# A 21st weight slot under the attention masks, the last projection items in two parts of 256 columns, and router products straight by token

## The chip, the core and the metric

The kernel runs on one core of a Trainium2 chip, in one launch. The metric is the device time of the program in microseconds (us), the median of the runs shown; lower is better. Inputs and weights are float32 in the device's memory (HBM), and the output is written back there.

## The reference

Two layers over 256 tokens of width 1024. Each layer first mixes tokens in three parallel branches and adds the result to x, then runs a mixture of experts on the new x. What matters here is the last projection, the router behind it, and the weights of 32 experts:

```python
merged = (gates[:, :, 0] * (oa @ w_proj_a[l]) + gates[:, :, 1] * (ob @ w_proj_b[l])
          + gates[:, :, 2] * (oc @ w_proj_c[l]))
x = x + merged @ w_out[l]                                 # w_out: 1024 x 1024
x = x + hier_moe(rms_norm(x, norm2_g[l]), w_router_group[l], w_router_expert[l],
                 w_expert_gate[l], w_expert_up[l], w_expert_down[l])

def hier_moe(h, w_rg, w_re, w_gate, w_up, w_down):        # h: 256 tokens x 1024
    pg = softmax(t @ w_rg)                                # 4 groups: the best one
    le = t @ w_re                                         # 8 experts in it: the best two
    hg, hu = t @ w_gate[e], t @ w_up[e]                   # 32 experts, each 1024 x 256
    return sum(silu(hg) * hu * weight @ w_down[e])        # and 256 x 1024
```

One expert's three matrices are 1 MB each, so a layer reads 96 MB of expert weights. Before the experts each layer reads some 46 MB for its projections.

## The kernel before

**Two stages in each layer.** The trunk (`trunk_stage`) does norm, projections and attention. The expert stage (`expert_stage`) does the router, then the experts in eight quads of four. Layer 0's trunk takes about the first 315 us, its expert stage lasts to about 524, and layer 1 repeats the two.

**The trunk's products.** Weights come in items of 1 MB through a ring of four slots in `arena`. An item is worked through in two half items, numbered j, so j = 88 to 91 are the last two items of `w_out` (items 44 and 45). To keep float32 accuracy, each half item is split: ScalarE (ACT) writes the rounded part `whi` (L811), VectorE (DVE) the remainder `wlo` in two halves (L991), and TensorE (PE) does three passes, L1295 to L1297. The half items of the last projection are `project_halves(84, 8, 4, ...)`: columns 0 to 511 of both token blocks first (j = 84 to 87), then columns 512 to 1023 (j = 88 to 91), twelve products of 512 columns each. When a block of 128 tokens by 512 columns is done, `x_out` adds it to `xs` (L1237) and raises `x_done`.

**The router.** `turn_new_x` (L545) transposes the new x, 8 transposes for each half of the columns. ACT and DVE scale the result into `h2t` (L521, L528). `router_half` (L556) multiplies the router weights `wr`, 64 columns wide and held in the array, by `h2t`, with even and odd blocks of k in the two halves of the array. This gives logits by expert, transposed, in two partial sums. DVE copies them (`logits_t`, L1633), and two products with `fold` (L1595) turn them by token and add the halves. `keep_clock` (L338) fills PE's time while DVE picks the experts (up to `sel`, L1655); the ranks follow (L1601 to L1606), then the one-hot tables, the gather of tokens (L1784, later L1824) and the gate and up products (L1797, later L1849; in the last quad L1871).

**The 20 slots of expert weights.** 12 slots lie in `arena` and 8 in `ring_rest`. The load number pos goes into slot pos % 20. The first 16 loads are issued inside the trunk as its data become free (`load_ahead`, by hand, between the projection items), four more when the last projection is done. From load 20 on (`quads_sp`, L470) each waits until the quad that used its slot is done: the first of them waits for `gate_up_pair(0)`. All these loads, and those of the trunk, are issued by SyncE (SP) in program order and share one queue. The last four loads of a layer are the down matrices of the last quad. The fourth comes in two halves, and `down_last` (L1889) multiplies in the order 0, 1, 2, 3. Right behind them in the queue stand the next layer's first items.

**The masks.** `mask_a` and `mask_c` are 1536 floats per partition, made once in layer 0 by DVE (L389 to L396) and read by the softmax of both layers (L1097). After the last softmax of layer 1 the final norm's gain is loaded into the same place.

## Time and profile before

| what | value |
| --- | --- |
| runs | 1054.49, 1053.40, 1053.19 us, median 1053.4 |
| profiled execution | 1054.47 us, of which the profile's span is 1052.8 |
| PE busy | 961.5 us (91% of the span) |
| DVE, ACT busy | 578.1 us (55%), 425.5 us (40%) |
| HBM read, written | 309.42 MB, 1.05 MB |
| granted TensorE clock, mean | 0.969 of 2.4 GHz |

Times in the rows further down are us from the start of the span. PE is the matmul engine and PEld its weight loads, which run beside the products. SPq is SyncE's sequencer while it issues a DMA; such a row tells when the transfer was issued and not when it landed. A record of PE is one pass: a float32 product or transpose of the text may be one or two records. "x8" behind a row is a merged run of eight. The bracket behind a row is the engine's idle time before it and what ended it.

### The profile page before, as it was taken

The page shows a single profiled execution, that of the slowest core. Times are in us where ns is not written, and L with a number is a line of the kernel's source. Part 1 is how long each engine was busy: PE and PEld are TensorE (multiplying, and loading weights), DVE is VectorE, ACT ScalarE, POOL GpSimd, SP SyncE. Part 2 cuts the span into 40 slices and gives each one's busy share as a digit, 9 for nine tenths or more (in the row PEclk, how much of TensorE's full clock was granted, in tenths as well). Part 3 has the DMA queues.
Part 4 walks back from the last instruction along what each step waited for, and adds up shares of the span by engine and source line. Part 5 has one row for each costly group of instructions (what it writes and reads, how often), then busy time and mean ns, then how long its engine had stood idle before and what let it go on. Part 6 is the DMA issues. An engine that isn't in the chain of part 4 may idle for free.

```text
span 1052.8 us, 15163 instructions
## 1 busy us (share of the span) xinstructions
PE 961.5 (91%) x5782; PEld 657.0 (62%) x5782; DVE 578.1 (55%) x1187; ACT 425.5 (40%) x905; POOL 58.5 (6%) x75
## 2 busy tenths in 40 slices
PE   8999999999999986977999999999999999776696
PEld 6788777777876432533588887777788754332343
DVE  7766788886864321211276568898869632122212
ACT  5434566666434110210353355666664421101122
POOL 1120400000010000000003004000000100000000
PEclk9999999999999998988999999999999999998898
DMA  9965544146899999999997664441569999999996
GB/s 339 349 203 184 188 126 135 62 129 237 306 408 401 420 421 416 419 421 421 409 381 239 198 199 160 125 137 61 154 225 379 418 388 421 421 419 419 421 420 257
DMA packets 96824, 311.43 MB, mean 296 GB/s; under 512 B 13392, under 2 KB 18544, under 8 KB 74224
## 3 DMA queue, kind: packets, MB, share of 16 engines
q1 hardware_dynamic: 96416, 310.47, 78.0%
q8 instruction: 43, 0.70, 0.3%
q14 instruction: 29, 0.24, 0.1%
q10 hardware_dynamic: 336, 0.02, 0.0%
HBM read 309.42 MB, written 1.05 MB: 295 GB/s over the span
## 4 chain that ended last, share of the span: by engine, by line
PE 63%; DMA 15%; SPq 8%; DVE 7%; ACT 4%; issue 3%; DVEq 0%; POOLq 0%; ACTq 0%
PE ps L1295 14%; PE ps L1297 14%; PE ps L1296 14%; DMA arena<-in_w_expert_up_dram 10%; SPq L470 7%; PE ps L1849 5%; DMA ring_rest<-in_w_expert_down_dram 5%; PE ps L1824 2%; PE ps L1393 2%; PE ps L1913 2%; DVE wlo L991 2%; PE ps L1401 2%; PE ps L1797 1%; ACT probs L886 1%; PE ps L1925 1%
## 5 line engine op out<-in xcount | busy, mean ns | idle before, releaser
L991 DVE TENSOR_TENSOR wlo<-arena,whi 128x512 fp32r<-128x512 f32 (+1 forms) x368 | 248.3, 714 | 98.1 <-ACT whi L811 95.7
L1295 PE MATMUL ps<-whi,ahi 128*128 128x512 f32 (+1 forms) x736 | 292.2, 397 | 6.6 <-DVE wlo L991 5.0
L1296 PE MATMUL ps<-wlo,ahi 128*128 128x512 f32 (+1 forms) x736 | 283.6, 385 | 0.0
L1297 PE MATMUL ps<-whi,alo 128*128 128x512 f32 (+1 forms) x736 | 283.5, 385 | 0.0
L811 ACT CAST whi<-arena 128x1024 fp32r<-128x1024 f32 (+1 forms) x184 | 189.1, 1030 | 200.6 <-PE ps L1297 199.7
L1295 PEld LDWEIGHTS ps<-whi,ahi 128*128 128x128 f32 x736 | 138.2, 188 | 41.9 <-DVE wlo L991 10.2
L1297 PEld LDWEIGHTS ps<-whi,alo 128*128 128x128 f32 x736 | 138.2, 188 | 28.4
L1296 PEld LDWEIGHTS ps<-wlo,ahi 128*128 128x128 f32 x736 | 138.5, 188 | 24.9
L1849 PE MATMUL ps<-ring_rest,rows 128*32 128x512 f32 x320 | 99.4, 669 | 30.2 <-DMA arena<-in_w_expert_up_dram 30.2
L1849 PE MATMUL ps<-arena,rows 128*32 128x512 f32 x448 | 99.4, 683 | 12.7 <-DMA arena<-in_w_expert_up_dram 7.5
L2041 DVE SCALAR_TENSOR_TENSOR acts<-ps,wslot,acts 128x256 f32<-128x256 f32 x16 | 7.7, 484 | 171.3 <-ACT acts L1759 148.0
L1759 ACT ACTIVATE acts<-ps,rslot 128x256 f32<-128x256 f32 x16 | 7.6, 475 | 171.4 <-PE ps L1849 168.5
L1824 PEld LDWEIGHTS ps<-onehot,work 128*128 128x128 f32 x448 | 53.4, 199 | 22.1 <-DVE onehot L2000 13.7
L1824 PE MATMUL ps<-onehot,work 128*128 128x128 f32 x448 | 56.0, 285 | 12.1 <-DVE onehot L2000 12.1
L1849 PEld LDWEIGHTS ps<-ring_rest,rows 128*32 128x32 f32 x320 | 23.7, 121 | 66.8 <-issue 66.8
L886 ACT ACTIVATE probs<-probs,neg 128x128 f32<-128x128 f32 x112 | 49.6, 444 | 33.1 <-DVE neg L1114 33.1
L1925 PE MATMUL ps<-rows,st 128*128 128x512 f32 x112 | 54.9, 612 | 0.2
L1849 PEld LDWEIGHTS ps<-arena,rows 128*32 128x32 f32 x448 | 24.4, 123 | 45.1 <-issue 45.1
L2025 DVE TENSOR_TENSOR xs<-ps,xs 128x512 f32<-128x512 f32 x56 | 38.7, 692 | 22.7 <-PE ps L1925 22.7
L1010 DVE SCALAR_TENSOR_TENSOR arena<-ps,rstd,arena 128x512 f32<-128x512 f32 (+2 forms) x68 | 46.7, 728 | 2.2 <-PE ps L1297 2.2
L1913 PE MATMUL ps<-arena,acts 128*32 128x512 f32 x256 | 43.6, 595 | 3.7 <-ACT acts L1763 3.7
L1913 PE MATMUL ps<-ring_rest,acts 128*32 128x512 f32 x192 | 36.3, 595 | 2.8 <-ACT acts L1763 2.8
(280 smaller groups left out, 970.2 us busy)
## 6 DMA issues: line engine op xcount, KB each, us to landing
arena<-in_w_in_dram SPq DMA_DIRECT2D x62, 1024.0 KB, 5.3
arena<-in_w_expert_gate_dram SPq DMA_DIRECT2D x36, 1024.0 KB, 25.5
arena<-in_w_expert_down_dram SPq DMA_DIRECT2D x32, 1024.0 KB, 22.8
arena<-in_w_expert_up_dram SPq DMA_DIRECT2D x32, 1024.0 KB, 26.2
ring_rest<-in_w_expert_down_dram SPq DMA_DIRECT2D x30, 1024.0 KB, 14.0
ring_rest<-in_w_expert_up_dram SPq DMA_DIRECT2D x24, 1024.0 KB, 27.2
ring_rest<-in_w_expert_gate_dram SPq DMA_DIRECT2D x20, 1024.0 KB, 26.5
arena<-in_w_proj_a_dram SPq DMA_DIRECT2D x8, 1024.0 KB, 5.0
```

The costliest lines, as they stand in the source:

```text
L470: sp.dma_start(slot, w[l, 4 * n + e].rearrange("(p k) f -> p (k f)", p=P)).then_inc(done, 16)
L811: act.copy(whi[:, jj % 2, 0:2 * w], half_slot(jj, w)).then_inc(hi_ready, 1)
L886: act.activation(probs[:, i, n, lo:hi], probs[:, i, n, lo:hi], ACT.Exp, bias=neg[:, i, tb, n:n + 1], accum_out=den[:, i, tb, n:n + 1])
L991: dve.tensor_tensor(wlo[:, jj % 2, cols], half_slot(jj, w)[:, cols], whi[:, jj % 2, cols].bitcast(F32), ALU.subtract).then_inc(low_split i ...
L1010: dve.scalar_tensor_tensor(out=z[:, tb, cols], in0=ps[:, bank + tb, 0:w], scalar=rstd[:, tb:tb + 1], in1=z[:, 0, cols], op0=ALU.mult, op1= ...
L1295: pe.matmul(o, hi, rhs_hi, start=first, stop=False)
L1296: pe.matmul(o, hi, rhs_lo, start=False, stop=False)
L1297: return pe.matmul(o, lo, rhs_hi, start=False, stop=last)
L1824: mm = pe.matmul(ps[:, 4 + k // 4, (k % 4) * QUAD:(k % 4 + 1) * QUAD], work[:, tb, k * P:(k + 1) * P], onehot[:, n % 2, tb, :], start=(tb ...
L1849: mm = pe.matmul(ps[e * EC:(e + 1) * EC, n % 2, :].rearrange("p (a f) -> p a f", a=2), xsel[:, k, e * EC:(e + 1) * EC], w, start=(k == 0), ...
L1913: mm = pe.matmul(ps[e * EC:(e + 1) * EC, 2 + nh, :], at_sb[:, kf, e * EC:(e + 1) * EC], w, start=(kf == 0), stop=(kf == 1), skip_group_che ...
L1925: pe.matmul(ps[:, 4 + tb, :], st[:, n % 2, tb * P:(tb + 1) * P], y[:, nh * BANK:(nh + 1) * BANK], start=True, stop=True).then_inc(R.back_r ...
```

## The change

The masks move into `spare_slot`, a buffer the size of one weight slot. In layer 0 the finished masks are written to device memory (`mask_store`). From the last softmax on, the buffer takes the down matrix of the layer's last expert; in layer 1 the masks are read back at the start of the trunk, and the cycle repeats. That load, number 95, leaves the end of the layer's queue. `down_last` takes it first, and the third matrix now comes in two halves. The gain of the final norm goes to an arena slot.

The load into slots 0 and 1 is issued at item 39 and no longer at item 42. The columns 512 to 1023 of the last projection are done as two parts of 256 columns, each through both items: j = 88, 89 for the first part, 90, 91 for the second, 24 products of 256 columns each. New x is therefore ready in steps (`x_done` 1 and 2, then 3 and 4, then 5 and 6), and it is transposed and sent to the router in parts of 4, 2 and 2 blocks of k (`X_PARTS`). The router products hold `h2t` in the array and stream the 36 columns of `wr`, so that logits come out by token; the copy, `fold` and its products go. `keep_clock` has one matmul less in two places.

```diff
-        mask_a = sb("mask_a", [P, 384])
-        mask_c = sb("mask_c", [P, 3, 384])
+        spare_slot = sb("spare_slot", [P, SLOT])
+        masks = spare_slot[:, 0:4 * 384]
+        mask_a = masks[:, 0:384]
+        mask_c = masks[:, 384:].rearrange("p (g c) -> p g c", g=3)
+        mask_store = nc.dram_tensor("mask_store", [P, 4 * 384], F32, kind="Internal").ap()
...
+        wr = sb("wr", [P, KB, WR])
...
+        gf = arena_slots[:, PLACES[16], 0:D]
...
+        WARM_SETUP, WARM_ROUTE, WARM_RANKS, WARM_LAST = 7, 7, 1, 1
...
+        def last_place(e):
+
+            return spare_slot[:] if e == 3 else places((LAST_DOWN - 3 + e) % RING_E)[:, 0, :]
+
         def load_last_down(sp, l, e):
 
-            slot = places((LAST_DOWN - 3 + e) % RING_E)[:, 0, :]
+            slot = last_place(e)
             src = w_expert_down[l, EXPERTS - 4 + e].rearrange("(p k) f -> p (k f)", p=P)
-            if e < 3:
+            if e != 2:
                 sp.dma_start(slot, src).then_inc(last_in[e], 16)
                 return
             for kf in range(2):
-                sp.dma_start(slot[:, kf * D:(kf + 1) * D], src[:, kf * D:(kf + 1) * D]).then_inc(last_in[3 + kf], 16)
+                sp.dma_start(slot[:, kf * D:(kf + 1) * D], src[:, kf * D:(kf + 1) * D]).then_inc(last_in[2 + 2 * kf], 16)
...
 
+        NARROW = 88
+
+        def turned_new(k):
+
+            bank = 5 if k == KB - 1 else 4 + k // 2
+            at = 0 if k == KB - 1 else (k % 2) * S
...
-        def turn_new_x(pe, nh):
-            pe.wait_ge(x_done, 2 * nh + 2)
-            for k in range(4 * nh, 4 * nh + 4):
+        X_PARTS = (range(0, 4), range(4, 6), range(6, 8))
+
+        def turn_new_x(pe, part):
...
+                pe.wait_ge(x_done, 2 * part + tb + 1)
+                for k in X_PARTS[part]:
+                    mm = pe.transpose(turned_new(k)[:, tb * P:(tb + 1) * P], xs[:, tb, k * P:(k + 1) * P], ident[:])
+                    if tb and k % 2:
+                        mm.then_inc(x_turned, 1)
...
+                pe.wait_ge(ahead_in, 16 * 3)
+            for k in X_PARTS[part]:
+                if k == 2 or k == KB - 1:
+                    pe.wait_ge(h2t_odd, 1 if k == 2 else 2)
+                elif k % 2 == 0:
+                    pe.wait_ge(h2t_ready, part + 1)
                 for tb in range(TB):
-                    at = (k % 2) * S + tb * P
-                    mm = pe.transpose(ps[:, 4 + k // 2, at:at + P], xs[:, tb, k * P:(k + 1) * P], ident[:])
...
-                               skip_group_check=True)
-            if nh:
-                mm.then_inc(logits_t_ready, 1)
+                    mm = pe.matmul(ps[:, 4, tb * 64:tb * 64 + WR], h2t[:, k, tb * P:(tb + 1) * P], wr[:, k, 0:WR],
+                                   start=(k == 0 and tb == 0), stop=(k == KB - 1), skip_group_check=True)
+            if part == 2:
+                mm.then_inc(logits_ready, 1)
...
-                ENDS = {71: 2, 75: 4, 77: 8, 80: 10, 83: 12, 87: 14}
+                ENDS = {71: 2, 75: 4, 77: 8, 80: 10, 83: 12, 87: 14, 89: 16}
...
+                            sp.wait_ge(before_me.y_ready, 2 * QUADS)
+                            sp.dma_start(masks, mask_store).then_inc(masks_in, 16)
+                        else:
+                            sp.wait_ge(masks_made, 1)
+                            sp.dma_start(mask_store, masks).then_inc(masks_out, 16)
...
+                                if l == 0:
+                                    sp.wait_ge(masks_out, 16)
+                                load_last_down(sp, l, 3)
                             if item == 38:
                                 sp.wait_ge(sv_ready, 1)
                                 sp.wait_ge(pv_mm, turned_before(BATCHES))
                                 load_ahead(18, 19)
+                            if item == 39:
+                                sp.wait_ge(obt_ready, 3)
+                                sp.wait_ge(o_lo, 5)
+                                load_ahead(0, 1)
                             if item == 42:
-                                sp.wait_ge(obt_ready, 3)
                                 sp.wait_ge(gated, 4)
-                                load_ahead(0, 1, 2)
+                                load_ahead(2)
                             if item == 43:
                                 sp.wait_ge(gated, 8)
                                 load_ahead(6, 4, 5)
...
                         load_ahead(11)
...
+                        sp.wait_ge(low_split, NARROW + 3)
                         load_ahead(8)
-                        sp.wait_ge(low_split, 2 * 46)
+                        sp.wait_ge(low_split, NARROW + 4)
                         load_ahead(9, 10)
...
+                            dve.wait_ge(masks_in, 16)
                         softmax_in(0)
...
+                        def x_narrow(c, tb):
+                            dve.wait_ge(quarter_ready, 14 + 2 * c + tb + 1)
+                            cols = slice(c * (BANK // 2), (c + 1) * (BANK // 2))
+                            to = quarter(xs, 2 + tb)[:, cols]
+                            dve.tensor_tensor(to, ps[:, 2 - 2 * c + tb, 0:BANK // 2], to, ALU.add).then_inc(x_done, 1)
...
+                        x_narrow(0, 0)
+                        x_narrow(0, 1)
                         low_at(91)
                         h2t_dve(dve, l, 1)
-                        x_out(2)
-                        x_out(3)
+                        x_narrow(1, 0)
+                        x_narrow(1, 1)
 
...
-                            for i in range(2 * pairs):
+                        def project_narrow(kb0, between):
+
+
+                            for i in range(4):
+                                j, (c, item) = NARROW + i, divmod(i, 2)
+                                if i in between:
+                                    between[i]()
+                                for kk in range(2):
+                                    pe.wait_ge(low_split if kk else low_first, j + 1)
+                                    for tb in range(TB):
+                                        for k in range(2 * kk, 2 * kk + 2):
+                                            at = slice(k * (BANK // 2), (k + 1) * (BANK // 2))
+                                            kb = 4 * item + k
+                                            mm = three_passes(ps[:, 2 - 2 * c + tb, 0:BANK // 2], kb0 + kb, tb, whi[:, j % 2, at], wlo[:, j % 2, at],
+                                                              kb == 0, kb == KB - 1)
+                                        if item and kk:
+                                            mm.then_inc(quarter_ready, 1)
+                                if item == 0:
+                                    mm.then_inc(conv_used, 1)
...
+                        project_halves(84, 8, 4, mt_lo, 8, {1: lambda: turn_merged(1)}, halves=1)
+                        pe.wait_ge(gated, 12)
+                        def first_parts_routed():
+                            turn_new_x(pe, 1)
+                            router_part(pe, 0)
+                        project_narrow(8, {2: lambda: turn_new_x(pe, 0), 3: first_parts_routed})
 
...
                 squares_act(act, 1)
...
             def route_pe(pe):
-                turn_new_x(pe, 1)
-                router_half(pe, 1)
-                pe.wait_ge(logits_t_evac, 1)
-                for tb in range(TB):
-                    mm = pe.matmul(ps[:, 1, tb * 64:tb * 64 + WR], logits_t[:, tb * P:(tb + 1) * P], fold[:],
-                                   start=(tb == 0), stop=True, skip_group_check=True)
-                mm.then_inc(logits_ready, 1)
+                router_part(pe, 1)
+                turn_new_x(pe, 2)
...
-                dve.wait_ge(logits_t_ready, 1)
-                dve.tensor_copy(logits_t, ps[:, 0, 0:S]).then_inc(logits_t_evac, 1)
                 dve.wait_ge(logits_ready, 1)
-                logits = ps[:, 1, 0:2 * 64].rearrange("p (t n) -> p t n", t=TB)[:, :, 0:WR]
...
             def load(sp, pos, done):
+                if pos == LAST_DOWN and done is expert_in:
+                    return
...
-                    for e in range(4):
-                        w = places(down_at(LAST, e) % RING_E)[:, 0, :]
+                    for e in (3, 0, 1, 2):
+                        w = last_place(e)
                         for kf in range(2):
-                            if e == 3 or kf == 0:
-                                pe.wait_ge(last_in[e + kf], 16 * (l + 1))
+                            if e == 2 or kf == 0:
+                                pe.wait_ge(last_in[e + 2 * kf], 16 * (l + 1))
                             for c in range(4):
                                 g = (e + c) % 4
                                 mm = pe.matmul(ps[g * EC:(g + 1) * EC, 2 + c // 2, (c % 2) * CQ_W:(c % 2 + 1) * CQ_W],
                                                at_sb[:, kf, e * EC:(e + 1) * EC], w[:, kf * D + c * CQ_W:kf * D + (c + 1) * CQ_W],
                                                start=(kf == 0), stop=(kf == 1), skip_group_check=True)
-                                if e == 3 and kf and c % 2:
+                                if e == 2 and kf and c % 2:
                                     mm.then_inc(R.y_ready, 1)
...
-                sp.wait_ge(quarter_ready, 16)
+                sp.wait_ge(quarter_ready, 18)
```

Where the change moves instructions on PE, at the end of a layer's trunk. Before, from the first transposes of new x on (`ident,xs` are transposes, `rows,wr` router products, `whi,ahi` and the like the projection, `mask_a,ident` is `keep_clock`):

```order
L545 MATMUL ps<-ident,xs 128x128 x8
L1295 MATMUL ps<-whi,ahi 128x512
...
L556 MATMUL ps<-rows,wr 64x256 x4
L1295 MATMUL ps<-whi,ahi 128x512
...
L545 MATMUL ps<-ident,xs 128x128 x8
L556 MATMUL ps<-rows,wr 64x256 x4
L1595 MATMUL ps<-fold,acts 128x36 x2
L338 MATMUL ps<-mask_a,ident 128x256 x8
```

The same place now:

```order
L556 MATMUL ps<-ident,xs 128x128 x8
L1354 MATMUL ps<-whi,ahi 128x256
...
L556 MATMUL ps<-ident,xs 128x128 x4
L569 MATMUL ps<-wr,rows 128x36 x8
L1354 MATMUL ps<-whi,ahi 128x256
...
L569 MATMUL ps<-wr,rows 128x36 x4
L556 MATMUL ps<-ident,xs 128x128 x4
L569 MATMUL ps<-wr,rows 128x36 x4
L340 MATMUL ps<-wr,ident 128x256 x7
```

Four transposes have moved ahead of the last half item, and eight router products in place of four stand there. Behind it stand eight router products and four transposes, where eight transposes, four router products and the two `fold` products stood.

On SP, the middle of layer 0's projection items before (`w_proj_c` is item 38, `w_proj_b` 39 to 41, `w_out` 42 to 45; the rest are expert loads):

```order
L705 DMA arena<-in_w_proj_c_dram 128x2x1024
L461 DMA ring_rest<-in_w_expert_gate_dram 128x2x512
...
L701 DMA arena<-in_w_proj_b_dram 128x4x512
L701 DMA arena<-in_w_proj_b_dram 128x2x512 x2
...
L701 DMA arena<-in_w_out_dram 128x4x512
L461 DMA arena<-in_w_expert_gate_dram 128x2x512
```

And now:

```order
L481 DMA spare_slot<-in_w_expert_down_dram 128x2048
L723 DMA arena<-in_w_proj_c_dram 128x2x1024
L461 DMA ring_rest<-in_w_expert_gate_dram 128x2x512
...
L719 DMA arena<-in_w_proj_b_dram 128x4x512
L461 DMA arena<-in_w_expert_gate_dram 128x2x512
L461 DMA arena<-in_w_expert_up_dram 128x2x512
L461 DMA arena<-in_w_expert_gate_dram 128x2x512
L461 DMA arena<-in_w_expert_up_dram 128x2x512
L719 DMA arena<-in_w_proj_b_dram 128x2x512 x2
```

The 21st slot's load stands ahead of item 38, and the 2 MB for slots 0 and 1 stand between items 39 and 40, where they stood behind item 42.

## Rows read from the trace of the kernel before

**Rows 1.** The page: share of the DMA engines, 40 slices of the span.

```profile
DMA  9965544146899999999997664441569999999996
```

**Rows 2.** Busy time by stretch: PE, PEld, DVE, ACT, POOL, then clock, DMA share, GB/s.

```profile
328.00:332.00 4.00, 4.00 (x35) 2.25 (x32) 0.00 (x0) 0.63 (x2) 0.00 (x0) 1.00 0.79 291
350.00:400.00 50.00, 45.66 (x336) 19.42 (x332) 10.54 (x22) 6.99 (x26) 0.00 (x0) 0.93 1.01 420
```

**Rows 3.** Order of time, SP: load 20, the first that waits for a quad.

```profile
328.33 0.80 SPq L470 DMA_DIRECT2D ring_rest<-in_w_expert_down_dram  x2
```

**Rows 4.** Order of time, end of layer 0's last quad: start, duration, engine, line.

```profile
512.80 0.41 PE L1871 MATMUL ps<-arena,rows 128*32 128x256 f32 x2 [0.65 <-DMA ring_rest<-in_w_expert_up_dram]
...
518.14 1.93 PE L1889 MATMUL ps<-ring_rest,acts 128*32 128x256 f32 x32
...
521.59 0.64 PE L1889 MATMUL ps<-ring_rest,acts 128*32 128x256 f32 x8 [0.21 <-DMA ring_rest<-in_w_expert_down_dram]
...
522.86 0.64 PE L1889 MATMUL ps<-ring_rest,acts 128*32 128x256 f32 x8 [0.64 <-DMA ring_rest<-in_w_expert_down_dram]
523.53 0.59 ACT L1769 CAST y_hi<-ps 128x512 fp32r<-128x512 f32 x1 [3.93 <-PE ps L1889]
```

**Rows 5.** The same in layer 1: the cast behind the last down product.

```profile
1041.95 0.59 ACT L1769 CAST y_hi<-ps 128x512 fp32r<-128x512 f32 x1 [3.90 <-PE ps L1889]
```

**Rows 6.** Order of time, PE, layer 0: from the transposes ahead of j = 90 to the last projection product.

```profile
307.13 1.04 PE L545 MATMUL ps<-ident,xs 128*128 128x128 f32 x8
...
307.92 0.48 PE L1295 MATMUL ps<-whi,ahi 128*128 128x512 f32 x1
...
310.87 1.08 PE L556 MATMUL ps<-rows,wr 128*64 128x256 f32 x8
...
311.88 0.50 PE L1295 MATMUL ps<-whi,ahi 128*128 128x512 f32 x1
...
314.55 0.39 PE L1297 MATMUL ps<-whi,alo 128*128 128x512 f32 x1
```

**Rows 7.** Order of time, PE: projection products of 256 columns earlier in layer 0.

```profile
226.30 0.28 PE L1295 MATMUL ps<-whi,ahi 128*128 128x256 f32 x1
...
227.25 0.28 PE L1297 MATMUL ps<-whi,alo 128*128 128x256 f32 x1
```

**Rows 8.** Order of time, layer 0: from the last new x to the picked experts.

```profile
314.29 1.38 DVE L1237 TENSOR_TENSOR xs<-ps,xs 128x512 f32<-128x512 f32 x2 [3.74 <-PE ps L1297]
...
316.42 0.84 ACT L521 ACTIVATE rows<-ps,gains 128x256 f32<-128x256 f32 x2 [5.82 <-PE ps L545]
...
317.31 1.20 PE L556 MATMUL ps<-rows,wr 128*64 128x256 f32 x8 [0.49 <-ACT rows L521]
...
319.04 0.63 PE L1595 MATMUL ps<-fold,acts 128*128 128x36 f32 x4 [0.53 <-DVE acts L1633]
...
319.71 0.17 DVE L1636 COPY lg<-ps 128x8 f32<-128x8 f32 x1 [0.73 <-PE ps L1595]
...
322.47 0.22 DVE L1655 TENSOR_TENSOR sel<-either,gmask 128x64 fp32r<-128x64 f32 x1
...
322.83 0.19 PEld L1601 LDWEIGHTS ps<-sel,before 128*128 128x128 f32 x1
```

**Rows 9.** Group by line: count, busy us, mean ns; short products with 128 x 128 weights.

```profile
L1836 PE MATMUL ps<-comb,onehot 128*128 128x5 f32 x64 | 8.1, 233 | 0.0
```

**Rows 10.** DMA issues of 284 to 288 us: count, KB, median us to landing.

```profile
arena<-in_w_out_dram SPq DMA_DIRECT2D x2, 1024.0 KB, 13.8
```

**Rows 11.** ACT in order of time: the casts of j = 16 and of j = 89.

```profile
53.73 1.05 ACT L811 CAST whi<-arena 128x1024 fp32r<-128x1024 f32 x1 [1.67 <-PE ps L1297]
...
301.34 1.05 ACT L811 CAST whi<-arena 128x1024 fp32r<-128x1024 f32 x1 [1.67 <-PE ps L1297]
```

**Rows 12.** DMA issues of 41 to 42 us: count, KB, us to landing.

```profile
arena<-in_w_in_dram SPq DMA_DIRECT2D x1, 1024.0 KB, 8.7
```

**Rows 13.** SP in order of time, at the end: the output, 1 MB in four stores.

```profile
1047.87 2.75 SPq L2184 DMA_DIRECT2D out_dram<-arena  x4
```

More of the change, by code:

```diff
@@ L526, in h2t_dve @@
             dve.wait_ge(x_turned, i + 1)
[L527 to L529 removed]
+            for k in (2 * i, 2 * i + 1)[1 if i == 3 else 0:]:
+                last = dve.tensor_scalar(h2t[:, k, :], turned_new(k), second_gain(l, k), None, ALU.mult)
             last.then_inc(h2t_odd, 1)
         def squares_act(act, nh):
[L533 to L534 removed]
+            act.wait_ge(x_done, 4 * nh + 2)
+            act.wait_ge(h2t_ready, 2 * nh + 1)
             for q in (2 * nh, 2 * nh + 1):
@@ L786, in split_at, with narrow_slot @@
                         return t[:, kb:kb + 2, :].rearrange("p k (t c) -> p k t c", t=TB)
+                    def narrow_slot(j, kk):
+                        c, item = divmod(j - NARROW, 2)
+                        blocks = ring[:, (NARROW // 2 + item) % RING, :].rearrange("p (k n) -> p k n", k=4)
+                        ks = slice(2 * kk, 2 * kk + 2) if kk is not None else slice(0, 4)
+                        return blocks[:, ks, c * (BANK // 2):(c + 1) * (BANK // 2)]
                     def half_slot(j, w):
```

73 lines of the change are left out of this document (37 added, 36 removed).

## The prediction

> **What bounds the kernel now.** I read the page's slices first [rows 1]. The DMA row shows two regimes in each layer. In the trunk it falls to 4 and below between slices 5 and 10: nothing more may be loaded there for want of free space. In the expert stage it stands at 9 from end to end. The windows confirm it [rows 2]: from 350 to 400 us the DMA share is 1.01 at 420 GB/s, while PE is busy 45.66 of 50. So an expert stage is as long as its transfers, from the moment when they may run freely to the last matrix and what PE does behind it. The window 328 to 332 shows a share of only 0.79: some 0.8 us without transfers, around the issue of load 20 at 328.33 [rows 3]. That is the first load that waits for a quad, so all slots are full and the queue is dry then. An expert stage thus starts at the first gate and up pair, which hangs on the router's chain, and ends behind the 96 MB less what was already loaded. PE must therefore save time in two places only: from the last projection product to that pair, and behind the last down matrix. The end of layer 0 [rows 4] gives the price of 1 MB: the two half matrices are taken at 521.59 and 522.86, 1.27 us apart, so one matrix is 2.54 us. The cast behind the last product starts at 523.53, and at 1041.95 in layer 1, where the wait is alike [rows 5].
>
> **The change, first part: one load fewer at the end.** Load 95 leaves the queue. The up weights ahead of the last down matrices land as before (512.80, where PE waited 0.65 for DMA), since nothing in front of them goes. Only the last matrix lands earlier, 2.54 us. Whether PE can follow: its down run starts at 518.14, tied to those up weights through activations and transposes, and 32 records take 1.93 there; a merged run of 8 takes 0.64 [rows 4]. The difference is 24 records in 1.29, 0.054 each. Now 64 can run without a wait: 1.93 + 32 x 0.054 = 3.65, to 521.8. The last half matrix would land at about 520.3, so PE decides. Before, the run ended at 522.86 + 0.64 = 523.50. The gain is **1.7 us** in a layer, the same in layer 1, because the spare slot is reloaded there after the last softmax. If PE kept up with DMA fully it would be 2.5, the upper bound; if something else in that slot's chain is late, nothing.
>
> **Second part: what fills earlier.** The load of the spare slot stands ahead of item 38 and the 2 MB for slots 0 and 1 ahead of item 40, in stretches where the DMA row of the page is low [rows 1]. They cost nothing where they stand if items 40 to 45 still land before their casts. Behind SP's new wait at item 39 are items 40 to 45 and all loads of experts; the semaphores it asks for come from work that is over about 9 us before item 40 is needed, by the empty slices. The last items gain: w_out's were 13.8 us on the way with expert loads ahead of them [rows 10], and 2 MB of those go (5.1 us). That is needed, since half item j = 89 now takes item 45, so by the cast at 301.34 [rows 11], where before j = 90 did, one half item later; issued at 284 to 288 and 13.8 us in transit gives 301.8 at the latest before, some 296 now. But earlier filling gives nothing of its own: the queue is dry before 328.33 already, and what has been loaded by then is 20 slots, now with the spare one.
>
> The mask store, 128 x 1536 x 4 bytes = 0.79 MB in layer 0, stands ahead of loads near item 9. That item's load is issued in the stretch 41 to 42 and is 8.7 us on the way [rows 12], so there at 49.8 or so; its cast is at 53.73 [rows 11]. The slack is 3.9. The store costs 0.79 x 2.54 = 2.0 at the load rate; at the output's rate (1 MB from 1047.87 to the span's end at 1052.8, at most 4.9 [rows 13]) it would be 3.9, just hidden. Nothing then, and 0 to 1 us as the bound above. Layer 1's read of the masks has the same kind of slack.
>
> **Third part: the route.** Ahead of the last projection product PE gets more work. A 256 column product takes 0.119: the eight steps from 226.30 to 227.25 [rows 7]. A half item is 24 x 0.119 = 2.86 plus about 0.1 of a wait, 2.95, where 12 products of 0.243 (11 steps from 311.88 to 314.55 [rows 6]) took 2.91: +0.15 over four half items. Four more transposes stand there (eight took 0.79, from 307.13 to 307.92, so 0.10 each [rows 6]): +0.4. Of the router, 8 products, each two records, stand there where four did, eight records in 1.01 (310.87 to 311.88 [rows 6]). The pitch of the new records, 36 columns long with 128 columns of weights, isn't in the trace. From below the transposes' 0.10 bound it (same weights, 128 columns streamed); from above the four `fold` records, 0.63 / 4 = 0.16 with a wait's lead in it [rows 8]. I take 0.12: 16 x 0.12 = 1.92, +0.9. One more switch between kinds of work, +0.1. Together **+1.55**.
>
> Behind it, the chain gets shorter. Before, the last product is streamed at 314.55 + 0.24 = 314.79 and the logits are read at 319.71 [rows 6, 8]: 4.92. Now: eight router records of the part before, 0.96 (the adds of new x run under them: before, they ended at 314.29 + 1.38 = 315.67, 0.88 after the product, at twice the width); four transposes and the hand-over, 0.75 as from 315.67 to ACT's start at 316.42; one ACT scale, 0.42 (half of 0.84), and 0.05; eight router records, 0.96, with 0.15 to drain; 0.04 to the reader. That is 3.33, so **-1.6**. The copy before `fold` (0.53 of PE idle) and `fold` itself are in the 4.92 [rows 8]. One warming matmul less: PE came to the ranks at 322.83, `sel` was done at 322.69 [rows 8], so **-0.1** of 0.14. The route's sum is -0.15, small between two large terms; at 0.10 a record it is -0.8, at 0.16 it is +1.1.
>
> A page of the Trainium skill speaks against this part. "TensorE: Matmul & The Clock Gate", section "LDWEIGHTS (loading the stationary operand)", says that a weight load costs by its columns, about 107 ns for 128, however few columns are then streamed. A product that streams only 36 columns is thus bound by its weights. By that figure 32 records take an estimated 3.4 us in place of 3.84, and the sum would be about 1048.9. The transposes' 0.10 agrees with it.
>
> **Sum.** -1.7 - 0.15 = -1.85 in a layer, -3.7 in two. The profiled execution took 1054.47; that gives 1050.8. It stands 1.1 above the median of the runs, 1053.4, so I forecast **1049.7**. What a measurement can tell from no change here is about 0.2%, 2.1 us.
>
> **Rivals.**
> - *The route comes later than that*, chance 0.22: the records go at 0.16, or the narrow products pay at each switch. +0.8 to +1.3 a layer, about 1052.0. The rows on `fold` speak for it, the transposes against.
> - *Tail or route give more*, 0.18: the down run follows the DMA, 2.5 in place of 1.7, or the records go at 0.10. -3.0 a layer, 1047.4. The 0.054 of rows 4 speaks against the first. The route alone can't give over about 1 us more: the loads behind the last projection product, issued near 316.5, four at 2.54, fill the queue to some 327, and t = 328.33 can't move ahead of that with profit.
> - *The weights of the router's short products are not loaded under the product before*, 0.04, the case on the slower side. A group of 64 short products of 5 columns with such weights has a mean of 233 ns [rows 9]. 32 records at 0.233 and not 0.12 are +3.6 a layer, so +1.75 in all, 1056.9. It decides from 0.18 a record (1.85 / 32 above 0.12), and is slower by over 0.2% from 0.21. Against it: the same group is busy 8.1 us for 64, 0.127 each, so they overlap.
> - *The early loads don't do what they should*, 0.06: item 45 or the masks land late, or the last matrix isn't what ended the layer. The tail's 1.7 is eaten, 1051 to 1054.
>
> The forecast itself has 0.50, for 1048.4 to 1050.8. Four in five lie between **1047.6 and 1052.2**. Faster than 1051.3 holds the forecast, the better case and a little of the others, 0.74; within 0.2% 0.21; slower 0.05.
>
> **What the profile of the changed kernel would show.** Layer 0's last down products as one run of 64 without a wait for DMA, ending near 521.8, and the cast about 1.7 earlier than now; with DMA waits still in it, the tail is mis-sized. Load 20 at about 328.2, with a short idle of DMA around it as now; if it is a microsecond later, the route's first term is larger. Router records at 0.12 behind one another; at 0.2, the slower rival. Projection products of 256 columns at 0.12. The casts of j = 16 and j = 89 without a wait for DMA. Layer 1's trunk shifted by 1.85, the end by 3.7. The forecast is wrong if the first stage from load 20 to the last matrix isn't shorter by one matrix, or if PE waits anywhere in the trunk for DMA where it doesn't now.

## The result, and the profile after

The changed kernel takes 1047.07 us (median of 1048.12, 1048.58, 1046.02 and 1045.76), the kernel before 1053.3 in the same comparison: a ratio of 0.9932, 95% interval 0.9920 to 0.9945. The medians are 6.2 us apart (which alone would be 0.9941, inside the interval), where 3.7 were forecast and 1047.6 was the lowest time of the range. Two later comparisons, each on one chip, gave 0.9920 (0.9906 to 0.9933) and 0.9924 (0.9911 to 0.9938), medians 8.9 and 8.4 us apart. The profiled execution took 1048.12 us, its span is 1046.4.

The end of layer 0's last quad in order of time, to be read beside [rows 4]:

```profile
513.67 0.41 PE L1950 MATMUL ps<-arena,rows 128*32 128x256 f32 x2 [2.09 <-DMA ring_rest<-in_w_expert_up_dram]
...
519.00 1.07 PE L1968 MATMUL ps<-spare_slot,acts 128*32 128x256 f32 x16
...
519.89 2.77 PE L1968 MATMUL ps<-ring_rest,acts 128*32 128x256 f32 x48
...
522.72 0.59 ACT L1848 CAST y_hi<-ps 128x512 fp32r<-128x512 f32 x1 [2.25 <-PE ps L1968]
```

The 64 records of the down run stand behind one another, with no wait for DMA: 3.66 us from 519.00 to 522.66, where the sum had 3.65. From the first up product to the cast it is 9.05 us (10.73 before), and in layer 1, from 1027.35 to 1036.40, 9.05 again (10.70 before, [rows 5]). But 513.67 stands 0.87 later than 512.80, though load 20 was issued 0.26 earlier and the same loads stand between the two.

PE, DVE and SP in order of time at the end of layer 0's trunk, beside [rows 6, 8]:

```profile
307.75 1.03 PE L556 MATMUL ps<-ident,xs 128*128 128x128 f32 x8
...
311.50 0.60 PE L556 MATMUL ps<-ident,xs 128*128 128x128 f32 x4
311.93 1.87 PE L569 MATMUL ps<-wr,rows 128*128 128x36 f32 x16
313.64 0.36 PE L1354 MATMUL ps<-whi,ahi 128*128 128x256 f32 x1
...
316.60 0.98 PE L569 MATMUL ps<-wr,rows 128*128 128x36 f32 x8
317.41 0.64 PE L556 MATMUL ps<-ident,xs 128*128 128x128 f32 x4
318.61 1.08 PE L569 MATMUL ps<-wr,rows 128*128 128x36 f32 x8 [0.56 <-ACT rows L533]
319.52 3.27 PE L340 MATMUL ps<-wr,ident 128*128 128x256 f32 x14
```
```profile
328.07 0.80 SPq L470 DMA_DIRECT2D ring_rest<-in_w_expert_down_dram  x2
```

Sixteen router records take 1.71 us (311.93 to 313.64), 0.107 each and not 0.12. From the streaming of the last projection product (316.60) to load 20 it is 11.47 us in layer 0 and 11.48 in layer 1, where it was 13.54 and 13.53; ahead of it PE needs 1.2 us more. So the route brings load 20 some 0.85 us forward in a layer (0.87 and 0.78). The page's DMA row, beside [rows 1], shows the trunk's emptiest slices and the full ones at the same places, and the window around load 20 a share of 0.86 for the 0.79 of [rows 2]:

```profile
DMA  9965633247999999999998556332588999999996
```
```profile
328.00:332.00 4.00, 4.00 (x38) 2.32 (x37) 0.00 (x0) 0.63 (x2) 0.00 (x0) 1.00 0.86 301
```

Laid out by stretch, after less before, the two executions differ like this (us):

| stretch | layer 0 | layer 1 |
| --- | --- | --- |
| trunk to the last projection product | +1.81, of which 0.62 stood there at the transposes already | +1.27 |
| from there to load 20 | -2.07 | -2.05 |
| load 20 to the first up product of the last quad | +1.13 | -2.31 |
| from there to the cast | -1.68 | -1.65 |
| cast to the end of the span | | -0.85 |

The first, second and fourth rows are the mechanism of the prediction. The third, -1.2 in sum, wasn't in it at all, nor the last. Windows of the expert stage (clock, DMA share, GB/s) give the first trace of why. Before, then after:

```profile
350.00:500.00 150.00, 0.90 1.01 419
870.00:1010.00 140.00, 0.90 1.01 420
```
```profile
350.00:500.00 150.00, 0.92 1.01 423
870.00:1010.00 140.00, 0.89 1.01 424
```

The engines are busy alike, at a share of 1.01, and move 1% more in the same time: 4 of 420 over a stream of some 186 us is 1.8 us a layer.

### The profile page after: what moved, and what is told of

It reads as the page before. It is cut to its first block, busy times and chain, and to the rows that moved or that the text cites. A ratio compares the mean times of both kernels' runs of the same rounds, so it can differ in the third digit from the quotient of the medians.

```text
span 1046.4 us, 15393 instructions
## 1 busy us (share of the span) xinstructions
PE 958.8 (92%) x5894; PEld 668.5 (64%) x5894; DVE 576.2 (55%) x1186; ACT 426.7 (41%) x907; POOL 58.1 (6%) x74
## 4 chain that ended last, share of the span: by engine, by line
PE 63%; DMA 16%; SPq 9%; DVE 6%; ACT 4%; issue 1%; DVEq 0%; ACTq 0%
PE ps L1354 14%; PE ps L1356 14%; PE ps L1355 14%; DMA arena<-in_w_expert_up_dram 10%; SPq L470 9%; DMA ring_rest<-in_w_expert_up_dram 5%; PE ps L1928 5%; PE ps L1452 2%; PE ps L1460 2%; PE ps L1903 1%; PE ps L1992 1%; PE ps L1876 1%; ACT probs L928 1%; DVE wlo L1038 1%; PE ps L1475 1%
## 5 line engine op out<-in xcount | busy, mean ns | idle before, releaser
L1354 PE MATMUL ps<-whi,ahi 128*128 128x512 f32 (+1 forms) x768 | 297.3, 387 | 6.5 <-DVE wlo L1038 5.1
L1356 PE MATMUL ps<-whi,alo 128*128 128x512 f32 (+1 forms) x768 | 289.6, 377 | 0.0
L1355 PE MATMUL ps<-wlo,ahi 128*128 128x512 f32 (+1 forms) x768 | 289.2, 377 | 0.0
L1038 DVE TENSOR_TENSOR wlo<-arena,whi 128x512 fp32r<-128x512 f32 (+1 forms) x352 | 231.5, 697 | 92.0 <-ACT whi L848 89.5
L848 ACT CAST whi<-arena 128x1024 fp32r<-128x1024 f32 (+1 forms) x176 | 180.6, 1029 | 186.5 <-PE ps L1356 186.5
L1354 PEld LDWEIGHTS ps<-whi,ahi 128*128 128x128 f32 x768 | 144.5, 188 | 38.0 <-DVE wlo L1038 7.9
L1356 PEld LDWEIGHTS ps<-whi,alo 128*128 128x128 f32 x768 | 144.4, 188 | 27.0
L1355 PEld LDWEIGHTS ps<-wlo,ahi 128*128 128x128 f32 x768 | 144.7, 188 | 24.4
L1928 PE MATMUL ps<-ring_rest,rows 128*32 128x512 f32 x320 | 95.2, 642 | 26.1 <-DMA arena<-in_w_expert_up_dram 26.1
L2096 DVE TENSOR_SCALAR rows<-ps,gain 128x128 f32<-128x128 f32 x56 | 15.8, 345 | 46.8 <-PE ps L1903 46.8
```

Source lines behind the costliest of these rows:

```text
L848: act.copy(whi[:, jj % 2, 0:2 * w], half_slot(jj, w)).then_inc(hi_ready, 1)
L1038: dve.tensor_tensor(wlo[:, jj % 2, cols], half_slot(jj, w)[:, cols], whi[:, jj % 2, cols].bitcast(F32), ALU.subtract).then_inc(low_split i ...
L1354: pe.matmul(o, hi, rhs_hi, start=first, stop=False)
L1355: pe.matmul(o, hi, rhs_lo, start=False, stop=False)
L1356: return pe.matmul(o, lo, rhs_hi, start=False, stop=last)
L1928: mm = pe.matmul(ps[e * EC:(e + 1) * EC, n % 2, :].rearrange("p (a f) -> p a f", a=2), xsel[:, k, e * EC:(e + 1) * EC], w, start=(k == 0), ...
```

## The experiments

Times are medians of four to eleven runs, with the ratio to the kernel before on the same chip and its 95% interval. "Place" is the address at which ring_rest begins in each partition of SBUF, which follows from the sizes of the buffers ahead of it.

**Both kernels again.** Two profiles of each, to see what belongs to the kernel.

> The kernel before, unchanged, to see what two profiles of one kernel differ by. Theory A (the two parts of the change explain the gain, the length of the transfer stream between load 20 and the last up matrices is the same in all kernels up to chance): ratio 1.000 within 0.001; from load 20 to the first product with the last up matrices 184.5 to 185.6 us in layer 0 and 182.6 to 185 in layer 1 in no fixed order, and the final products again at a pitch of 0.21 us. Theory B (the change itself makes layer 1's stream 2.3 us shorter, because the queue isn't dry for so long at load 20): layer 1 again at 184.5 or more here.

> The changed kernel, unchanged. Ratio to before 0.993 to 0.9955 in both theories. Theory A: the stream from load 20 to the last up matrices is again somewhere from 182.6 to 185.6 us, independent of the layer. Theory B: about 182.6 in layer 1 again and shorter than before's by 2. Both: final products at 0.12 us.

Measured: 1054.25 us, 0.9995 (0.9985 to 1.0005), and 1045.86 us, 0.9920. The rate again was 419 and 420 GB/s in the one and 424 and 424 in the other. So the rate goes with the kernel, in both layers; the length of the stream scatters by more (from load 20 to the start of the last down run 190.9, 188.0, 187.9 and 189.5 us in four layers of the changed kernel), so that theory B as I put it, for layer 1 alone, falls.

**The route without the slot.** The edit takes out the load at item 37, the masks' store and load, and puts load 95 back:

```diff
-            return spare_slot[:] if e == 3 else places((LAST_DOWN - 3 + e) % RING_E)[:, 0, :]
+            return places((LAST_DOWN - 3 + e) % RING_E)[:, 0, :]
...
-                    for e in (3, 0, 1, 2):
+                    for e in range(4):
```

> The changed kernel without the 21st slot: load 95 comes last again, in its old slot and in halves, the masks stay where they are made, nothing is stored or read back. What is left is the route and the early loads. Theory A: the route gives 0.85 a layer, so 1.7 in all, ratio 0.9984; load 20 as in the changed kernel, the tails as before (10.7 us from the first up product to the cast), the final products at a pitch of 0.21. Theory B: 1.7 and the 2 us of layer 1's stream, so 3.7, ratio 0.9965. A theory C, that the spare slot gives nothing and the route everything: 0.994.

Measured: 1051.06 us, 0.9967 (0.9955 to 0.9980), and 424 GB/s. With neither the slot nor its loads the rate is still the higher one.

**Projection items in whole halves of 512 columns**, slot and router by token kept, new x turned and routed in two parts of four blocks:

```diff
-                        project_narrow(8, {2: lambda: turn_new_x(pe, 0), 3: first_parts_routed})
+                        project_halves(84, 8, 4, mt_lo, 8, {1: lambda: turn_merged(1), 6: lambda: turn_new_x(pe, 0), 7: lambda: router_part(pe, 0)})
```

> The changed kernel with the last projection items in halves of 512 columns again, as before, and new x routed in two parts; the router products stay by token, the spare slot stays. It tells what the narrow parts give. Theory A: ahead of the last product four transposes and eight records fewer (-1.25 with the part of 256 columns), behind it four transposes and sixteen records in place of four and eight, one more ACT scale and a wider add: 4.9 - 0.5 (no copy) - 0.55 (no fold) + 0.5 = 4.3 to 4.5 against 3.13, so load 20 about as late as in the changed kernel or 0.3 us later, ratio 0.993 to 0.9955 to before, within 0.001 of the changed kernel. A rival, that the narrow parts carry the route's gain: load 20 later by 0.8 us a layer, ratio higher by 0.0015.

Measured: 1049.40 us, 0.9950 (0.9933 to 0.9966), 3.5 us above the changed kernel on that chip. In layer 1 load 20 comes 12.89 us behind the last product, 1.4 more than with narrow parts, about as worked out (4.3 to 4.5 for 3.13). But ahead of that product, from the cast of layer 0 on, only 0.55 us were saved (309.96 for 310.51), and not 1.25. So load 20 comes 0.85 later in all, which is the rival's 0.8: the narrow parts carry the route's gain. In layer 0 the stretch behind the last product is 15.98. There TensorE's clock fell; windows of PE in layer 0 (busy, count, granted clock, DMA share, GB/s):

```profile
316.00:317.00 1.00, 0.54 (x5) 1.00 1.31 393
317.00:318.00 1.00, 0.56 (x6) 1.00 0.52 188
318.00:319.00 1.00, 0.95 (x9) 0.97 1.08 451
319.00:320.00 1.00, 1.00 (x7) 0.50 0.97 393
```

Ahead of the fall PE was idle 0.78 us for x and 0.49 for the scaling. The fourteen warming records behind the router then take 5.77 us in place of 3.27. With narrow parts PE has eight router records to do in the first of these gaps.

**The place of ring_rest.** 423 or 424 GB/s in four profiles of three kernels that have the same buffers (the changed one, no_spare and wide), where two profiles of the kernel before had 419, led to this. Before, ring_rest begins at byte 144672, 32 above a multiple of 256; after, at 145152, a multiple. One line of unused bytes moves it. This is the line in the kernel before; in the changed kernel it is [P, 8] for 32 bytes and [P, 16] for 64:

```diff
+        sb("pad_rest", [P, 120])
         with ExitStack() as ctx:
             ring_rest = sb("ring_rest", [P, (RING_E - RING_A) * SLOT], F32, ctx)
```

> The kernel before with 480 unused bytes per partition ahead of ring_rest, and nothing else. In it ring_rest, where 8 of the 20 slots lie, begins at byte 144672 of a partition, 32 above a multiple of 256; in the changed kernel and its variants it begins at 145152, a multiple of 256, because other buffers changed size. Here it begins at 145152 too. Two profiles of the kernel before show 419 GB/s from 350 to 500 us, four of the changed kernel and its variants 423 or 424. Theory P (the place of ring_rest does that): 423 to 424 GB/s here, 1.5 to 2 us off each layer's stream, ratio 0.9962 to 0.9975. Theory Q (something else in the change does it, the order of the loads or the router): 419 GB/s and a ratio of 1.000.

> The kernel before with ring_rest moved up by 480 bytes, once more, on the same chip as the next three, which it is the base of. Ratio 0.9950 to 0.9970.

> The changed kernel with 32 unused bytes ahead of ring_rest, so that it begins at 145184, again 32 above a multiple of 256 as in the kernel before. Theory P: 419 GB/s in the expert stage and 3 to 4 us more than the changed kernel, ratio to before 0.9955 to 0.9965, which leaves the change proper with 3.7 to 4.7 us. Theory Q: 424 GB/s and a ratio of 0.992 to 0.994 as in the changed kernel.

> The changed kernel with 64 unused bytes ahead of ring_rest, which then begins at 145216, a multiple of 64, 64 above one of 256. If what counts is a multiple of 64: 424 GB/s and the ratio of the changed kernel, 0.992 to 0.993. If it is a multiple of 256: 419 GB/s and 0.995 to 0.9965, as with 32.

Measured: the kernel before with ring_rest at 145152 takes 1051.48 us, 0.9958 (0.9945 to 0.9972), and 1050.65, 0.9963 (0.9948 to 0.9977), on another chip. The changed kernel with 32 bytes more takes 1050.66, 0.9951 (0.9937 to 0.9964), with 64 bytes more 1049.29, 0.9955 (0.9939 to 0.9971). The same windows, of before_shift and then of after_off:

```profile
350.00:500.00 150.00, 0.91 1.01 424
870.00:1010.00 140.00, 0.89 1.01 424
```
```profile
350.00:500.00 150.00, 0.91 1.01 419
870.00:1010.00 140.00, 0.89 1.01 420
```

Unused bytes alone turn the rate on and off, in both kernels. In the kernel before 3.9 us go with it; in the changed one, whose two places were never timed on the same chip, 1.7 to 3.7 us by the ratios (0.9920 to 0.9932 against 0.9948 to 0.9955). The time is lost in the stream: from load 20 to the start of the last down run it is 189.8, 190.3, 189.9 and 190.0 us in the four layers of before and before_again, and 188.0, 188.3, 188.1 and 188.1 in those of before_shift and before_shift_b, 1.9 less a layer. The first of before_shift goes from 329.72 to 517.68, where the kernel before has 328.33 and 518.14 [rows 3, 4]:

```profile
329.72 0.80 SPq L471 DMA_DIRECT2D ring_rest<-in_w_expert_down_dram  x2
...
517.68 3.05 PE L1890 MATMUL ps<-ring_rest,acts 128*32 128x256 f32 x48
```

The unused bytes move every buffer behind ring_rest too, but between 350 and 500 us the weight loads go to ring_rest and arena alone, and arena lies ahead of it.

Theory P holds. 64 above a multiple of 256 is as bad as 32 (420 GB/s), so a multiple of 64 isn't enough. Whether it must be one of 256 isn't shown: 128 above was not tried, and a multiple of 128 would fit all these runs as well.

The Trainium skill, DMA: Bandwidth & Descriptors, section How a descriptor splits into AXI transactions, has a descriptor that doesn't start at a multiple of 256 bytes, here a row of 8 KB, pay for one more transaction. It says so of what is read, and here it is the side written that is off. The direction agrees; the size doesn't: for rows of 8 KB, 32 bytes off, in 8 of 20 slots, that is an estimated 0.16%, and 1.1% was measured.

**Arena and the spare slot too**, which begin 160 and 32 bytes above a multiple:

```diff
+        sb("pad_arena", [P, 24])
...
+        sb("pad_spare", [P, 32])
...
+        sb("pad_rest", [P, 8])
```

> The changed kernel with unused bytes ahead of arena, of the spare slot and of ring_rest, so that all three begin at multiples of 256 (33024, 135168, 145408; arena was 160 above one, the spare slot 32). Theory P: the 12 slots in arena gain as the 8 in ring_rest did, or more: 428 to 436 GB/s in the expert stage, 3 to 8 us off the changed kernel, ratio to before 0.985 to 0.990. By the Trainium skill, DMA: Bandwidth & Descriptors, section How a descriptor splits into AXI transactions, a row of 8 KB that starts 160 bytes above such a multiple costs an estimated 261 beats for 256, so 2% of the slots in arena, 1.2% in all. Theory Q: as the changed kernel, 0.992 to 0.994.

> The changed kernel, for comparison on the same chip: ratio to before 0.991 to 0.9935, 423 to 424 GB/s in the expert stage.

> The changed kernel with arena, spare slot and ring_rest all at multiples of 256. If each place costs as much as ring_rest's did for its share of the slots (4.5 GB/s for 8 of 20), arena's 12 would give 7 GB/s and 5 us; the first run of it showed 1.5 to 2 GB/s more, which is 0.4% of two stages of 185 us, 1.5 us. I expect 0.8 to 1.6 us under after_third, 425 to 426 GB/s.

Measured: 1045.73 us, 0.9905 (0.9890 to 0.9921). On one chip the changed kernel took 1046.43, 0.9924, and this one 1045.39, 0.9908 (0.9894 to 0.9921), at 424 and 426 GB/s. It is the fastest version of the study, 1 us ahead of the changed kernel, which the intervals don't separate. Going by the rates, 2 GB/s for 4 to 5, arena's place costs a fraction of what ring_rest's did, though it holds 12 of the 20 slots; the 1.2% estimated by the Trainium skill's rule isn't there. Why, is open.

**The slot alone.** The kernel before with the slot, the masks' store and load, and the new order of the last down run; route and items as before. Ring_rest lies 192 above a multiple of 256 here (420 and 421 GB/s), so the kernel before is its base:

```diff
                                 sp.wait_ge(pv_mm, turned_before(BATCHES))
+                                if l == 0:
+                                    sp.wait_ge(masks_out, 16)
+                                load_last_down(sp, l, 3)
```

> The kernel before with the 21st slot alone: masks in it, stored and read back, load 95 issued at item 38, its matrix taken first in the last down run. Route, router and projection items as before. To make room the ranks, big and the softmax's small sums lie in other buffers, which changes no work; ring_rest begins at 145856, a multiple of 64 and not of 256. Theory T (the tail gives 1.7 us a layer as in my sum): 3.4 us under the kernel before with ring_rest in the same state, so ratio 0.9925 to 0.994 if 64 is enough for the rate of 424 GB/s, 0.9965 if it isn't. From the first up product of the last quad to the cast 9.05 us in place of 10.7. Rival: the matrix that is no longer in the queue gives its whole 2.5 us, ratio 0.991 or 0.995.

> The 21st slot alone, once more. Theory R (load 20 earlier by 0.85 us a layer, the end follows): 1.7 us above the run before. Theory S (the route's gain is lost in transfers that start later ahead of load 20): within 0.7 us of it.

Measured: 1050.99 us, 0.9967 (0.9953 to 0.9980), and 1050.82, 0.9959 (0.9946 to 0.9973): 3.5 and 4.3 us, for a forecast of 3.4. The stretch from the last down run's start to the cast is 3.72 and 3.71 us, for 5.39 and 5.37 before. The rival of 2.5 a layer (5.0) lies just outside the first interval and inside the second; the profiles decide against it, since the down run is one without waits.

**Does the route's gain arrive?** Four pairs of runs ask it, the first without the slot and the others with it, each pair with ring_rest in an equally good or bad place.

> The changed kernel without the 21st slot, once more. Its ring_rest begins at 145152, so it differs from the run before by the route and the early loads alone. Theory R (load 20 is issued 0.85 us earlier in a layer and the end follows): 1.7 us under the run before, ratio lower by 0.0016. Theory S (the route's gain isn't passed on, since the last loads ahead of load 20 are issued 1.3 to 1.8 us later and the transfer engines then idle at 312 to 320 us for what they no longer idle at 328): ratio as in the run before within 0.0007.

> The changed kernel with ring_rest 32 bytes above a multiple of 256, once more: base of the next three on this chip. Ratio 0.9945 to 0.996.

> As after_off_b, with eleven keep_clock products in place of seven between the router and the ranks. They run behind the pick, 4 more of 0.22 to 0.24 us: load 20 0.9 us later in each layer, back to where the kernel before has it or 0.05 behind. Theory R: 1.8 us above after_off_b. Theory S: under 0.7 above it, since the transfers ahead of load 20 are the limit.

> As after_off_b, with the 2 MB for slots 0 and 1 issued behind item 42 again, as in the kernel before. Item 45 is needed at j = 89 and its load then stands behind 2 MB more, 5.1 us. My prediction had early loads worth nothing of their own and needed only for item 45, which before landed at 301.8 at the latest against a cast at 301.9 now: 0 to 0.5 us a layer, so 0 to 1 us above after_off_b, a wait for DMA at that cast if any. Theory S would have it lose more, up to 2 us, because the queue then holds its last loads later.

| pair on one chip | us | the route gives |
| --- | --- | --- |
| before_shift_b, no_spare_b | 1050.65, 1050.60 | 0.0 |
| tail, after_64 | 1050.99, 1049.29 | 1.7 |
| tail_b, after_off_b | 1050.82, 1050.35 | 0.5 |
| after_off_b, route_plus | 1050.35, 1052.39 | 2.0, for load 20 later by 1.49 in each layer |

A product of keep_clock is two records, so that the four are eight and my 0.9 was 1.49. Of 3.0 us given back at load 20, 2.0 arrived by the medians. By the ratios to the kernel before (0.9963 and 0.9959, 0.9967 and 0.9955, 0.9959 and 0.9948, 0.9948 and 0.9976) the four pairs differ by 0.4, 1.3, 1.2 and 3.0 us. So how much of the route's 1.7 arrives these pairs don't tell: the two reckonings differ by up to 1.0 us, and the medians of the kernel before by 0.8 from chip to chip.

The profiles show that part of it is lost, as theory S had it, and where. When load 20 is issued earlier, the stream behind it gets longer. From load 20 to the last down run the four layers of no_spare and no_spare_b have 190.5, 188.9, 189.6 and 188.8 us, 1.3 more on average than those of before_shift and before_shift_b. With ring_rest off, the six layers of after_off, after_64 and after_off_b have 190.1 on average, and the four of tail and tail_b 189.5. That is 0.6 to 1.3 us a layer of a gain of some 0.85, with a scatter from layer to layer of the same size.

A place for the loss can be seen. Windows of SP (clock, DMA share, GB/s) of the changed kernel, and of late01:

```profile
312.00:314.00 2.00, 1.00 0.90 332
318.00:320.00 2.00, 1.00 0.86 299
328.00:330.00 2.00, 1.00 0.80 221
```
```profile
312.00:314.00 2.00, 1.00 1.03 430
318.00:320.00 2.00, 1.00 0.98 410
328.00:330.00 2.00, 1.00 0.91 311
```

The last loads ahead of load 20 are issued up to 1.8 us later than before, at 316.79 against 314.97, and the queue runs dry in front of them too. In after_off_b, from which late01 differs by the early loads alone, the three shares are 1.00, 0.86 and 0.71. late01 issues 2 MB later, has them in the queue at that point and fills the last two gaps, and takes 1049.85, 0.9950 (0.9937 to 0.9964), against 1050.35, 0.9948. So the early loads bring nothing, and filling the gaps with bytes that could have been moved before brings nothing either, at least nothing that these intervals show. The casts of j = 88 and 89 wait for no DMA in it, at 299.18 and 301.90.

**The clock at the end.** In the kernel before, the final products of layer 1 ran at half clock in one profile and at full in the next.

```diff
+                            if e == 3 and not hands_over:
+                                keep_clock(pe, 1, LAST % 2)
...
+                    if not hands_over:
+                        keep_clock(pe, 5, LAST % 2)
```

> The kernel before with keep_clock products in layer 1's last down run, one ahead of each half of the fourth matrix, and five behind the run, where PE waits 1.4 us for y_lo. It tells what the clock at the very end is worth. Of the two profiles of the kernel before, one shows the final products at a pitch of 0.21 us and a clock of 0.70 and 0.50 from 1042 to 1046, the other 0.12 and 1.00, so the clock there falls in some executions alone. If the fall is a cost of the kernel before: ratio 0.9990 to 0.9998, and from the cast of y_hi to the end 10.0 us in place of 10.85. If it isn't worth a microsecond: ratio 1.000 within 0.0008.

Measured: 1056.12 us, 1.0008 (0.9998 to 1.0017). The clock stays at 1.00, but five products are ten records and last 2.43 us, where the gap has 1.4:

```profile
1043.62 2.43 PE L338 MATMUL ps<-mask_a,ident 128*128 128x256 f32 x10
1045.70 0.47 PE L505 MATMUL ps<-y_hi,st 128*128 128x256 f32 x1
```

From the cast to the end it is 10.68 us. So what was won was given back, and the run doesn't price the clock. The profiles do. With the slot, thirteen profiles of eight kernels have 9.9 to 10.1 us there. Without it, of seven profiles with load 95 last two have 10.0 and 10.1, and five 10.4 to 10.9 (one of these is before_warm). Windows of PE in the kernel before:

```profile
1040.00:1042.00 2.00, 1.28 (x16) 1.00 0.31 123
1042.00:1044.00 2.00, 0.69 (x3) 0.70 0.00 0
1044.00:1046.00 2.00, 2.00 (x11) 0.50 0.00 0
```

PE was busy 1.28 and 0.69 of 2 us ahead of the fall, since the down run waited for its matrices. With the slot the run has no gaps. That is up to 0.85 us, of which the slot alone's 3.5 and 4.3 may hold some.

## Why the prediction was wrong

**The last matrix: right, in mechanism and size.** PE bounds the tail, one run of 64 without waits, 3.66 us for 3.65; 1.68 and 1.65 us off, for 1.7. The slot alone measured 3.5 and 4.3 for 3.4.

**The step that failed** is in the first part: "The up weights ahead of the last down matrices land as before (512.80, where PE waited 0.65 for DMA), since nothing in front of them goes." With it went the premise of the whole sum, that the stream of loads takes as long before and after; the effect of a buffer's place stood in no term of it. The change alters the sizes of mask_a, wr, fold and rk, and with them where ring_rest lies; the stream went from 419 to 424 GB/s. before_shift shows 3.9 us for that alone, in the kernel before, and the changed kernel without it (after_off, after_64, after_off_b) is 4.7 to 5.3 us under the kernel before, ratios 0.9948 to 0.9955. In that state it would have stood inside the range, at its lower end. The change proper then gives somewhat more than the 3.7 of the sum, though after_64's interval holds 3.7 as well: 3.4 for the slot, and the rest from the route and the clock at the end, which these runs don't part. The two layers of the first profile hide the effect: +1.13 and -2.31 in the third row of the table, with a scatter of some 2 us over it.

**The route: mis-sized, with the right signs.** Ahead of the last product 1.2 us for 1.55: the records go at 0.107 and not at 0.12, so that sixteen for eight cost 0.70 and not 0.9, and the 0.1 for a switch isn't there. The 107 ns of the Trainium skill (TensorE: Matmul & The Clock Gate, LDWEIGHTS) were the better price. Behind it 2.06 for 1.7: the logits are read 3.13 us after the last product (319.73) for 3.33, and keep_clock has lost a product in its second place too, between ranks and gather, which I left out: PE reaches the gather at 324.10 for 324.46 before. Load 20 is thus 0.85 us earlier and not 0.15. Of these 1.7 us in two layers, 0 to 1.7 arrived. The cap that I named, that load 20 can't profit from standing ahead of the loads before it, points the same way.

**The clock at the end** wasn't in the sum: up to 0.85.

**Costed at nothing, and right:** the early loads (late01), the masks' store and load, item 45 at j = 89. The 0.62 us by which layer 0's trunk is late stands at the first cast already (7.88 for 7.33) and goes with when the first weights land.

**The rivals.** The slower one, short products that don't overlap their weights, is out: 0.107 a record. The better case named the route's records, and its time, 1047.4, was near the measured one by luck. Its -3.0 a layer comes out of none of its terms either: with the sum's other terms kept, the first gives 2.65, the second 2.5 and both 3.3.

## What to carry to other kernels

Where a stage is bound by transfers, look at where their targets begin: a buffer resized anywhere ahead of them moves them, and a few unused bytes that bring them to a multiple of 256 may be worth as much as the change itself (here 3.9 us beside 4.7 to 5.3). Before costing an edit in such a stage, compare the GB/s of the same window in both kernels, at equal DMA share; when it differs, undo it by padding and only then price the rest. Taking a load off the end of the queue is worth what PE behind it can follow, and time won ahead of a full queue doesn't all arrive: look whether the stream behind it gets longer (here by 0.6 to 1.3 us a layer, for some 0.85 won).

## What the runs showed of the hardware

- HBM to SBUF in the expert stage, at a DMA share of 1.01: 419 to 421 GB/s with ring_rest 32, 64 or 192 bytes above a multiple of 256 in each partition (before, before_again, before_warm, after_off, after_64, tail), 423 to 424 on a multiple, 425 to 426 with all three buffers on one. In the kernel before that is 3.9 us of 1054.5. 128 above a multiple was not measured.
- Router products of 36 columns with 128 x 128 weights run at 0.107 us a record.
- The granted clock fell from 1.00 to 0.50, 2.4 to 1.2 GHz, behind waits of PE that didn't always have such an end: in wide in layer 0, behind waits of 0.78 and 0.49 us (and not in its layer 1, with 0.79 and 0.49), and at the end of the kernel before, behind gaps in the down run (and not in before_again).
